# Sparse attention stage of a two-block transformer kernel: accumulation of head pairs in one half of the output partitions, and the reciprocal of a unit's sum as a power on GpSimd

## The reference

```
for each token tile t (128 tokens), head h of group g, branch b (selected, window):
    s = q[h, tile t] @ k[b, g].T + causal mask          # 128 x (t+1)*128
    e = exp(s - max(s));  z = sum(e)
    p = e / z * gate[b, tile t, h]
    o[h, tile t] += p @ v[b, g]                         # on top of the compressed branch
y = o @ w_out                                           # 1024 x 1024
```

## Time and profile before

| | us |
|---|---|
| median of 3 runs | 1943.6 (1942.14 to 1944.35) |
| the profiled execution, its own time | 1943.83 |
| its span | 1942.0 |
| PE busy | 1831.9 (94%) |
| PEld busy | 1518.6 (78%) |
| DVE busy | 680.8 (35%) |
| ACT busy | 701.7 (36%) |
| POOL busy | 786.0 (40%) |
| TensorE clock granted, mean over the span | 0.976 |

### The profile page before, as it was taken

How to read it: one execution, slowest core, us unless ns; L and a number is a source line. 1 busy time by engine, 2 the same in 40 slices (tenths; PEclk the granted TensorE clock), 3 DMA queues, 4 the chain that set the end, 5 groups by cost and what they waited for, 6 DMA issues and landing times. The chain is left out here.

```text
span 1942.0 us, 23391 instructions
## 1 busy us (share of the span) xinstructions
PE 1831.9 (94%) x9070; PEld 1518.6 (78%) x9070; DVE 680.8 (35%) x1238; ACT 701.7 (36%) x1355; POOL 786.0 (40%) x472
## 2 busy tenths in 40 slices
PE   6999999999999999999899978878999999999998
PEld 5988776778877888888688877766887778888886
DVE  2543334341532110110355368883302343303322
ACT  3233434232333321232444246663433333313332
POOL 3443322324434444444346234443461234444542
PEclk8999999999999999999999889999999999999999
DMA  6322121113343323332234130002351222333331
GB/s 215 88 77 65 44 60 42 47 54 95 109 152 87 98 93 92 98 97 98 87 102 135 44 87 1 1 1 87 100 150 55 65 77 87 96 100 98 97 105 49
DMA packets 222878, 161.88 MB, mean 83 GB/s; under 512 B 9768, under 2 KB 197296, under 8 KB 222768
## 3 DMA queue, kind: packets, MB, share of 16 engines
q1 hardware_dynamic: 221712, 159.32, 27.8%
q10 hardware_dynamic: 1056, 1.06, 0.2%
HBM read 156.15 MB, written 2.11 MB: 81 GB/s over the span
## 5 line engine op out<-in xcount | busy, mean ns | idle before, releaser
L300 POOL TENSOR_TENSOR w_low<-ring,w_high 128x1024 fp32r<-128x1024 f32 (+2 forms) x303 | 682.2, 2257 | 935.2 <-ACT w_high L292 935.2
L313 PE MATMUL psum<-hT,w_high 128*128 128x512 f32 x1232 | 491.8, 399 | 9.8 <-PEq L177 6.1
L314 PE MATMUL psum<-hL,w_high 128*128 128x512 f32 x1232 | 485.0, 394 | 0.0
L315 PE MATMUL psum<-hT,w_low 128*128 128x512 f32 x1232 | 485.0, 394 | 0.0
L292 ACT ACTIVATE w_high<-ring 128x1024 fp32r<-128x1024 f32 (+2 forms) x303 | 296.8, 981 | 507.4 <-PE psum L315 507.3
L313 PEld LDWEIGHTS psum<-hT,w_high 128*128 128x128 f32 x1232 | 235.0, 191 | 63.8 <-issue 11.6
L315 PEld LDWEIGHTS psum<-hT,w_low 128*128 128x128 f32 x1232 | 234.2, 190 | 50.1
L314 PEld LDWEIGHTS psum<-hL,w_high 128*128 128x128 f32 x1232 | 234.9, 191 | 47.1
L313 PE MATMUL psum<-w_high,hT 128*128 128x512 f32 (+2 forms) x384 | 132.9, 346 | 7.2 <-PEq L2410 3.6
L313 PE MATMUL psum<-w_high,ffn_act 128*128 128x512 f32 x352 | 139.1, 395 | 0.0
L315 PE MATMUL psum<-w_high,ffn_act 128*128 128x512 f32 x352 | 138.9, 395 | 0.0
(11 more groups left out here) (362 smaller groups left out, 2554.3 us busy)
## 6 DMA issues: line engine op xcount, KB each, us to landing
ring<-in_w_in SPq DMA_DIRECT2D x58, 512.0 KB, 3.8
ring<-in_ffn_w_up SPq DMA_DIRECT2D x44, 512.0 KB, 3.8
ring<-in_w_gate SPq DMA_DIRECT2D x22, 512.0 KB, 3.9
ring<-in_w_up SPq DMA_DIRECT2D x22, 512.0 KB, 3.9
ring<-in_w_down SPq DMA_DIRECT2D x20, 512.0 KB, 3.6
ring<-in_ffn_w_down SPq DMA_DIRECT2D x20, 512.0 KB, 3.7
ring<-in_nsa_w_in SPq DMA_DIRECT2D x18, 512.0 KB, 3.8
ring<-in_ca_wkv SPq DMA_DIRECT2D x16, 512.0 KB, 3.9
```

Of the source, the lines that this page charges most:

```text
L300: nc.gpsimd.tensor_tensor(tile_view(w_low, n, SPLIT), tile_view(ring, n, RING), tile_view(w_high, n, SPLIT), ALU.subtract).then_inc(w_lo, 1)
L313: nc.tensor.matmul(ps, lhsT=sh, rhs=mh, start=first, stop=False)
L314: nc.tensor.matmul(ps, lhsT=sh, rhs=ml_, start=False, stop=False)
L315: return nc.tensor.matmul(ps, lhsT=sl, rhs=mh, start=False, stop=last)
```

## The change

Three things are done, the third to make the first possible.

1. Both heads of a pair go to the same half of `oT`'s partitions, half hp, in the two neighbouring chunks 2g and 2g+1. The four additions of 64x128 become two of 64x2x128. `vcmp` is filled in the same placing.
2. The rows of `w_out` are permuted on the host to match (`chunk_heads`), as another permutation already is.
3. The reciprocal on DVE goes. POOL raises each unit's sum to the power -1 (128x1, the exponent in a column of `stat`), waits for its own result, and then scales the unit. It waits for each unit's exponential by itself, where before it waited once per pair for the reciprocal. `p_inverted` counts units now; ACT's wait for it keeps its distance.

```
@@ (new function)
+def chunk_heads(weight):
+
+    m = weight.reshape(NSA_G, 2, 2, HD, -1)
+    return np.ascontiguousarray(m.transpose(0, 2, 1, 3, 4).reshape(weight.shape))
@@ (DVE, before the stage)
             for i in range(HPG):
-                ins = nc.vector.tensor_copy(vcmp[32 * i:32 * i + 32, :, i * HD:(i + 1) * HD],
+
+                at_ = (i % 2) * P + (i // 2) * HD
+                ins = nc.vector.tensor_copy(vcmp[32 * i:32 * i + 32, :, at_:at_ + HD],
                                             bank[7][0:32, P:P + 256].rearrange("p (g d) -> p g d", d=HD))
@@
+        minus_one = stat[:, 36:37]
@@ (ACT)
                         if i == 0 and s >= 3:
-                            a.wait_ge(p_inverted, s - 2)
+                            a.wait_ge(p_inverted, 2 * s - 4)
@@ (DVE)
-                if s < n_np:
-                    v.wait_ge(p_exped, 2 * s + 2)
-                    if s >= 3:
-                        v.wait_ge(p_scaled, 2 * s - 4)
-                    nc.vector.reciprocal(np_recip[s % 3], np_total[s % 3]).then_inc(p_inverted, 1)
                 if s >= 4 and s % 2 == 0:
 
                     o = (s - 4) // 2
                     g, t, hp, _ = npairs[2 * o]
                     v.wait_ge(p_summed, 2 * o + 2)
-                    halves = [(oT[HD * i:HD * i + HD, 2 * g + hp, q_tile(t)], sum_of(o)[:, i * P:(i + 1) * P]) for i in range(2)]
-                    for dst, src in halves:
-                        ins = nc.vector.tensor_tensor(dst, src[0:HD], dst, ALU.add)
-                    link(ins)
-                    for dst, src in halves:
-                        ins = nc.vector.tensor_tensor(dst, src[HD:P], dst, ALU.add)
-                    ins.then_inc(p_added, 1)
+                    dst = oT[HD * hp:HD * hp + HD, 2 * g:2 * g + 2, q_tile(t)]
+                    src = sum_of(o).rearrange("p (h c) -> p h c", c=P)
+                    link(nc.vector.tensor_tensor(dst, src[0:HD], dst, ALU.add))
+                    nc.vector.tensor_tensor(dst, src[HD:P], dst, ALU.add).then_inc(p_added, 1)
@@ (POOL)
+            nc.gpsimd.memset(minus_one, -1.0).then_inc(zeroed, 1)
+            g_.wait_ge(zeroed, 3)
             for v_ in range(2 * n_np):
                 g, t, h, kb = unit_of(v_)
                 wd = (t + 1) * P
-                if v_ % 2 == 0:
-                    g_.wait_ge(p_inverted, v_ // 2 + 1)
-                nc.gpsimd.tensor_scalar(nprob[:, v_ % 6, 0:wd], nprob[:, v_ % 6, 0:wd], np_recip[v_ // 2 % 3][:, v_ % 2:v_ % 2 + 1],
+                p, i = v_ // 2, v_ % 2
+                g_.wait_ge(p_exped, v_ + 1)
+                nc.gpsimd.tensor_tensor(np_recip[p % 3][:, i:i + 1], np_total[p % 3][:, i:i + 1], minus_one,
+                                        ALU.pow).then_inc(p_inverted, 1)
+                g_.wait_ge(p_inverted, v_ + 1)
+                nc.gpsimd.tensor_scalar(nprob[:, v_ % 6, 0:wd], nprob[:, v_ % 6, 0:wd], np_recip[p % 3][:, i:i + 1],
                                         gates[:, t, h, 1 + kb // 4:2 + kb // 4], ALU.mult, ALU.mult).then_inc(p_scaled, 1)
@@ (host)
+    send['nsa_w_out_2'] = chunk_heads(send['nsa_w_out_2'])
```

## The result

| | us |
|---|---|
| median of 5 runs of the changed kernel | 1932.5 (1931.5 to 1935.0) |
| median of the runs of before beside them | 1943.2 (1942.1 to 1944.4) |
| ratio, with its 95% interval | 0.9949 (0.9934 to 0.9963) |
| the profiled execution, its own time / its span | 1932.52 / 1930.7 |
| the stage, from the first scores to the last addition | 171.9 (1139.05 to 1310.95), before 183.4 |

The change gains 10.7 us, 0.5%. I had forecast 28. The stage became 11.5 us shorter, so the time was won where it was expected, and it is the size that is off. PE starts the next block 2.3 us behind the last addition, as before.

The account below looks back on a forecast made before the run. PE was taken to bound the kernel, DVE's order the stage. PE's floor 148.2 us plus 7 us of hand-offs made the stage 155 us, 28 us less: 1943.83 - 28, less 0.2, gave 1915.6 us, range 1906 to 1943.

Parts of the forecast that it names:

- What set the stage before: DVE's fixed order: 26.3 us waiting for exponentials ahead of the reciprocal delays `nprobL`, for which PE waits 35.2 us.
- I take p = 0.30 us: Time of each of 128 powers on POOL; with w, its 0.10 us wait for its own result, POOL totals 135.3 us.
- three limits near 147 us: In the changed stage PE, DVE and POOL each limit at about the same time, near 147 us.
- The sum by width: Larger of POOL's and DVE's time per pair, 16 pairs of each of four widths: 146 us for the stage.
- the hand-offs: Between nearly full PE, DVE and POOL: 0.11 us for each of 64 pairs, about 7 us added to the stage.
- the first rival: POOL becomes the bound over the whole stage, 1923 us at p = 0.46, a gain up to p = 0.6; chance 0.10.
- The signs I had named: Trace marks for right (no DVE exponential wait, `nprobL` waits under 10 us) or wrong (POOL without ACT waits, DVE idle again).
- PE's floor: The stage without PE's waits for `nprobL`: 183.4 - 35.2 = 148.2 us.
- The additions: On DVE, 64 of 256 columns at 0.417 us, 26.7 us instead of 36.3, so 9.6 us saved.
- The wait for PE's sum: DVE's additions might next be late for PE's sum; not counted as a loss, but DVE's gain not taken in full.
- The ring of waits: Low parts, ACT's copy, transposes and scaled units still wait on each other: about 14 us gained, 1930 us; chance 0.08.
- The pause at the first power: POOL's first power pays a pause of its own, up to 5.95 us, giving 1921.6 us; chance 0.03.

Follow-up runs that it names:

- power_alone: Kernel before, with only the reciprocal on DVE replaced by powers on POOL; old placing of heads and four additions kept: 1932.6 us.
- adds_alone: Changed kernel with the reciprocal back on DVE as before, keeping the additions in their new form and the new placing of heads: 1936.5 us.
- late_recip: Changed kernel without the power; the reciprocal is on DVE, behind the additions of its step instead of ahead of them: 1922.5 us.
- split_adds: late_recip with the two additions of an output dealt out over the even and the odd step, one ahead of each reciprocal: 1915.3 us.
- next_recip: split_adds with each reciprocal on DVE made one step later, right behind the next pair's maxima: 1911.9 us.
- mult_for_power: Changed kernel with a multiplication in place of POOL's power, so it does not compute the layer: 1905.8 us.
- pair_power: Changed kernel with one 128x2 power on POOL for both sums of a pair in place of two of 128x1: 1916.9 us.

## Why the prediction was wrong in size

**What set the stage before: right.** That most of PE's wait for `nprobL` was made of DVE's reciprocal waiting for ACT is shown twice. Taken off DVE, in the change and power_alone, PE's wait falls from 35.2 to 2.1 and 4.2 us. Moved on DVE, with the additions as wide as in adds_alone, DVE's wait goes from 27.8 there to 16.3, 8.2 and none in late_recip, split_adds and next_recip, and 7.8, 22.5, 28.7 and 33.3 us are off the stage.

**The step that failed: "I take p = 0.30 us".** The power measures 0.550 us, with w = 0.10 as taken. I had bounded p from above by an addition of 128x128 (line 1663), 460 ns, and allowed for arithmetic that no row showed only by doubling the fixed part. The fixed part was about right: 0.14 extrapolated, 0.190 measured. The power's arithmetic is another 0.36 us and made the instruction of one column dearer than the addition of 128. The row was no upper end for an operation of another kind. This put 128 x 0.25 = 32 us more on POOL than the sum had, and my forecast of three limits near 147 us became one limit, POOL. The case that came, p between 0.46 and 0.65 with POOL as the bound, had only 0.10 of the chance.

**The sum by width: near with the measured p, in part by luck.** With p + w = 0.65, POOL needs 2.20, 2.41, 2.62 and 2.84 us for a pair. With the larger of POOL and DVE my working gives 16 x (2.20 + 2.41 + 2.62 + 3.01) = 164 us and 171 with the hand-offs; measured 171.9. That it comes so near is luck in its terms: it takes DVE's 3.01 for the widest pairs, where the trace has POOL without a wait too, it leaves out the 7.7 us of splits on POOL, and it adds 7 us of hand-offs of which POOL's timeline shows none. What the trace shows is POOL at work for 165.0 us on end, with 6.9 us ahead of and behind it. It is the first rival, POOL as the bound over the whole stage.

**The signs I had named.** DVE's wait for the exponentials went, the additions take what I had put, and PE's wait for `nprobL` is under 10 us. But a power starts 0.65 us ahead of its scaling, not 0.3 to 0.5, and both signs of being wrong came. POOL is busy without waits for ACT while PE's weight loads wait for it in 58 places. DVE's idle time reappeared at about its old size, 15.0 us of it ahead of the low parts and the rest ahead of the maxima. That this idle time is made of POOL's lateness is shown by mult_for_power, where the same two waits of DVE, 15.0 and 13.4 us in the change, are 4.6 and 3.0 us.

**PE's floor and the hand-offs: not far off.** I had added 7 us to a floor of 148.2, for hand-offs that had no row of their own. With a shorter instruction on POOL than I had taken (mult_for_power) the stage is 146.3 us, so 148.2 was no floor: it took only PE's waits for `nprobL` as recoverable. With POOL's total at 135.8 us, close to my 135.3, pair_power's stage is 154.3 us against my 155, though there the first unit of a pair waits for the second. A power of 0.30 us was not run; an estimate from these two stages is a gain of 29 to 37 us.

**The additions: right in price, not in effect.** 412 and 427 ns against 417 taken. Alone they bring 7.8 us of the 9.4, in the change nothing, because POOL is the bound there. My sum put them into DVE's relief, which the other limits cut; that they would be cut to nothing follows only with the longer power (power_alone).

**The wait for PE's sum: harmless.** DVE waits 2.1 us for it ahead of the additions in the whole stage, and 1.3 us of the same kind stood in the earlier trace rows already. **The ring of waits** is excluded by pair_power: a ring that holds whatever POOL is relieved of can't give 15.6 us for it. **The pause at the first power** did not come; the first one and its scaling:

```profile
1141.70 0.55 POOL L2408 TENSOR_TENSOR stat<-stat 128x1 f32<-128x1 f32 x1 [5.41 <-ACT nprob L2361]
1142.36 0.46 POOL L2411 TENSOR_SCALAR nprob<-nprob,stat,ngate 128x128 f32<-128x128 f32 x1
```

It starts 0.15 us behind the end of ACT's read of the sum (1141.55 us) and takes 0.55 us like the others (542 to 567 ns over all 128), and the scaling starts 0.11 us behind it. The Trainium skill, "GPSIMD Engine Reference", section "Instruction dispatch", says that a first call of freshly loaded code pays about 6 us. No call in this stage shows such a pause; whether the power's code was freshly loaded at that point, no row shows.

## What to carry to other kernels

When an engine with a fixed order waits in it for another engine, first look for work of its own that can stand ahead of the wait, or move the waiting instruction behind the next independent one: here that took 25.5 us off the stage beyond what the wider additions had given (175.6 to 150.1), where moving the instruction to another engine gave 3.7 beyond them (175.6 to 171.9). Rows of other operations give no upper bound for an operation whose arithmetic no row shows. When an engine takes on 128 of them, work out at which price it becomes the bound, and give the prices beyond that point their share of the chance. Gains on an engine that is no longer the bound do not add: wider additions were worth 7.8 us alone and nothing beside the power.

## What the runs showed of the hardware

- On GpSimd a power of 128x1 takes 550 ns and one of 128x2 takes 700 ns, a multiplication of 128x1 190 ns. The second column costs 150 ns more, so one power for two sums is cheaper than two powers; wider ones were not run.
- A multiplication of 128x1 on GpSimd holds the engine for 0.14 to 0.15 us by start-to-start distance, less than its 190 ns in the profile; a dose of 128 of them moved the stage by 18.2 us.
- GpSimd's wait for the result of its own last instruction costs 0.10 us each time (13.3 us for 128).
- An addition on VectorE that reads PSUM and SBUF takes 412 to 427 ns for 64x256 (the change), against 273 to 294 ns for 64x128 (before).
